# Making the attention gates as one more projection block, turned afterwards, in a two-layer hybrid decoder step on one core

## What is computed

```python
def nsa_project(h, pos, w_in, b_gate, g_q, g_k):
    z = h @ w_in
    q = z[..., :NSA_QD].reshape(B, T, NSA_HEADS, HEAD_DIM)          # 1024 columns
    kv = z[..., NSA_QD:NSA_QD + 6 * NSA_KVD].reshape(...)           # 1536 columns
    gates = jax.nn.sigmoid((z[..., NSA_QD + 6 * NSA_KVD:] + b_gate).astype(jnp.float32))   # 48 columns
    q = partial_rope(rms_norm(q, g_q), pos)
    ...
```

## Times and profile before

| | us |
|---|---|
| median of 3 executions | 2009.44 |
| lowest, highest | 2008.98, 2014.61 |
| the profiled execution | 2014.1 |
| its span, first to last instruction | 2012.3 |
| PE busy in it | 1832.8 (91%) |
| DVE, ACT, POOL busy | 895.4, 677.2, 444.4 |
| mean granted PE clock, of full | 0.929 |

### The profile page before, as it was taken

The page is one execution under the profiler, slowest core; times in us unless marked ns, Lnnn a source line. Parts: engine busy times, 40 slices in busy tenths (PEclk is TensorE's granted clock), DMA queues, the critical chain, the costliest instruction groups (busy, mean ns, idle before and its releaser), DMA issues.

```text
span 2012.3 us, 32814 instructions
## 1 busy us (share of the span) xinstructions
PE 1832.8 (91%) x13711; PEld 1661.6 (83%) x13711; DVE 895.4 (44%) x1345; ACT 677.2 (34%) x1129; POOL 444.4 (22%) x380
## 2 busy tenths in 40 slices
PE   4999997999999997999799999788876999999996
PEld 2989876999999997889678878566653999999996
DVE  6060254744434455546522422777522644444343
ACT  3243333332323233232333321666652331313130
POOL 3344224100000003433222121576812100000000
PEclk8999767999999998999898898799997999999998
DMA  4122122222222221322312110000283122222211
GB/s 158 43 84 84 45 88 88 108 102 85 84 85 84 85 89 45 106 74 95 126 53 84 43 53 1 1 1 9 91 339 149 57 113 103 107 85 85 85 43 43
DMA packets 22255, 166.28 MB, mean 83 GB/s; under 512 B 2112, under 2 KB 9840, under 8 KB 12568
## 3 DMA queue, kind: packets, MB, share of 16 engines
q1 hardware_dynamic: 17896, 122.60, 16.4%
q0 software_dynamic: 4208, 41.45, 5.5%
HBM read 154.00 MB, written 10.04 MB: 82 GB/s over the span
## 4 chain that ended last, share of the span: by engine, by line
PE 79%; DVE 9%; ACT 4%; POOL 3%; issue 2%; DMA 2%; ACTq 0%; DVEq 0%; SPq 0%; PEldq 0%; POOLq 0%
PE slot L2029 51%; PE slot L2253 11%; POOL phase L908 3%; PE slot L2240 2%; PE slot L2001 2%; PE slot L2103 1%; ACT phase L1349 1%; PE slot L2135 1%; DVE normed_x L1460 1%; PE slot L2064 1%; PE slot L2376 1%; DVE phase L1444 1%; PE slot L2436 1%; PE slot L2081 1%; DVE phase L1861 1%
## 5 line engine op out<-in xcount | busy, mean ns | idle before, releaser
L1179 ACT ACTIVATE w_high<-weights 128x1024 fp32r<-128x1024 f32 x128 | 135.3, 1060 | 258.1 <-PE slot L2029 250.0
L2029 PE MATMUL slot<-h_high,w_high 128*128 128x260 f32 x1024 | 209.6, 286 | 6.6 <-issue 6.6
L2029 PE MATMUL slot<-h_high,w_rest 128*128 128x260 f32 x1024 | 209.3, 286 | 5.6 <-issue 5.6
L2029 PE MATMUL slot<-h_rest,w_high 128*128 128x260 f32 x1024 | 208.4, 285 | 0.0
L2029 PE MATMUL slot<-u_high,w_high 128*128 128x260 f32 x1024 | 206.3, 283 | 0.0
L2029 PE MATMUL slot<-u_rest,w_high 128*128 128x260 f32 x1024 | 206.1, 283 | 0.0
L2029 PE MATMUL slot<-u_high,w_rest 128*128 128x260 f32 x1024 | 206.0, 283 | 0.0
L1640 DVE TENSOR_TENSOR w_rest<-weights,w_high 128x1024 fp32r<-128x1024 f32 x128 | 156.0, 1222 | 31.1 <-ACT w_high L1179 31.1
L2029 PEld LDWEIGHTS slot<-h_high,w_high 128*128 128x128 f32 x1024 | 160.4, 191 | 10.8 <-issue 10.5
L2029 PEld LDWEIGHTS slot<-h_high,w_rest 128*128 128x128 f32 x1024 | 160.2, 191 | 3.1 <-issue 3.1
L2029 PEld LDWEIGHTS slot<-h_rest,w_high 128*128 128x128 f32 x1024 | 160.0, 191 | 0.0
(11 more groups left out here) (354 smaller groups left out, 3780.5 us busy)
## 6 DMA issues: line engine op xcount, KB each, us to landing
weights<-in_wt SPq DMA_DIRECT2D x47, 2048.0 KB, 8.6
weights<-in_state SPq DMA_DIRECT2D x2, 2048.0 KB, 8.7
out<-weights POOLq DMA_DIRECT2D x2, 2048.0 KB, 8.7
weights<-in_w SPq DMA_DIRECT2D x2, 2048.0 KB, 9.0
phase<-in_v_win SPq DMA_DIRECT2D x4, 1024.0 KB, 6.9
out<-phase SPq DMA_DIRECT2D x6, 512.0 KB, 6.5
phase<-in_x_prompt SPq DMA_DIRECT2D x2, 1024.0 KB, 6.3
weights<-in_k_win SPq DMA_DIRECT2D x2, 1024.0 KB, 7.1
```

Source lines behind the costliest of these rows:

```text
L1179: nc.scalar.activation(w_part[k % 4][0][:, :, :], ring[:, s, :, 128 * (k % 4):128 * (k % 4) + 128], ACT.Copy).then_inc(w_high_ready, 1)
L2029: last = mm(ps[0:w.shape[2], a, 0:HT], w[:, k, :], m[:, k, HT * a:HT * a + HT], start=k == 0 and w is high and m is x_high, stop=k == DC - ...
```

## The change

The gates become a 21st block of the projection, 48 outputs wide: ACT and POOL split `wgate` into the two `pw_part[0]` buffers, PE makes "gt" with 48 matmuls of 260 columns from `u_part`, ACT copies the [48, 520] result to `z4`, and PE turns it back with five transposes ("gates") into the form that it had. Both stand after sw(18) and nm(19); "gt" comes before sw(19), "gates" after it. Since `u_part` is now read until gt is through, the first cache rows go where `hT` lay (free once the split tokens are made), the first gather moves up to step 6 of the projection, and the rounded compression weights go to `no` in exchange.

```diff
-        rows16 = [cols("no", 0, 4096), W(0, 4096)]
+        rows16 = [cols("hT", 0, 4096), W(0, 4096)]
-        w1_part = [part("w1_high", at["hT"][0], 16, 256), part("w1_rest", at["ring"][0], 16, 256)]
+        w1_part = [part("w1_high", at["no"][0], 16, 256), part("w1_rest", at["ring"][0], 16, 256)]
...
                 if n < len(chunks):
                     yield "z", n
-                elif n == len(chunks):
-                    yield "gates", 0
                 if 0 <= n - 2 < len(chunks) and is_roped[n - 2]:
                     yield "sw", n - 2
                 if 0 <= n - 1 < len(chunks) and is_roped[n - 1]:
                     yield "nm", n - 1
+                if n >= len(chunks) and n < len(chunks) + 2:
+                    yield ("gt", "gates")[n - len(chunks)], 0
...
# POOL
+                if n == len(chunks):
+                    nc.gpsimd.tensor_tensor(pw_part[0][1][:, :, 0:48], wgate, pw_part[0][0][:, :, 0:48].bitcast(F32),
+                                            ALU.subtract).then_inc(pw_rest_ready, 1)
+                    return
...
-                if what == "z" and n + 2 < len(chunks):
+                if what == "z" and n + 2 <= len(chunks):
                     projection_rest(n + 2)
+                    if n == 6:
+                        pool.wait_ge(mixed_rest_ready[0], DC)
+                        pool.wait_ge(mixed_rest_ready[1], DC)
+                        pool.wait_ge(rows_known, 1)
+                        rows_load(0)
...
-                elif what == "gates":
-                    pool.wait_ge(rows_known, 1)
-                    last_z = where(("z", len(chunks) - 1))
-                    pool.wait_ge(full[last_z[0]], last_z[1] + 1)
-                    rows_load(0)
+                elif what == "gt":
+                    pool.wait_ge(full[where(("gt", 0))[0]], where(("gt", 0))[1] + 1)
...
                     if (r, sp) == (0, 2):
                         pool.wait_ge(roped, turned[len(chunks)])
+                        pool.wait_ge(full[where(("gates", 0))[0]], where(("gates", 0))[1] + 1)
                         rows_load(1)
# ACT
+                if n == len(chunks):
+                    act.wait_ge(nsa_small_in, 32)
+                    nc.scalar.activation(pw_part[0][0][:, :, 0:48], wgate, ACT.Copy).then_inc(pw_high_ready, 1)
+                    return
...
             root_of(len(chunks) - 1, k_roots)
+            ps, fr = await_product(act, ("gt", 0))
+            act.wait_ge(roped, turned[len(chunks) - 3])
+            nc.scalar.activation(halves(z4[0:48, 0, :]), tok(ps)[0:48, :, :], ACT.Copy).then_inc(z_ready, 1)
+            act.wait_ge(z_ready, len(chunks) + 1)
+            act.sem_inc(fr, 1)
# PE
+                elif what == "gt":
+                    pe.wait_ge(pw_rest_ready, len(chunks) + 1)
+                    ps, fu = claim(pe, ("gt", 0))
+                    split_products(ps, [w[:, :, 0:48] for w in pw_part[0]], u_part).then_inc(fu, 1)
                 elif what == "gates":
-                    pe.wait_ge(nsa_small_in, 32)
+                    pe.wait_ge(z_ready, len(chunks) + 1)
                     ps, fu = claim(pe, ("gates", 0))
                     for t in range(5):
                         rows = 128 if t < TT else NS
-                        for k in range(DC):
-                            last = mm(ps[0:rows, 0, 48 * t:48 * t + 48], hT[:, k, 128 * t:128 * t + rows], wgate[:, k, :],
-                                      start=k == 0, stop=k == DC - 1)
+                        last = nc.tensor.transpose(ps[0:rows, 0, 48 * t:48 * t + 48], z4[0:48, 0, 128 * t:128 * t + rows],
+                                                   ident[0:48, 0:48])
                     last.then_inc(fu, 1)
```

More of the change, by code:

```diff
@@ L510, in trunk @@
         for what, n in steps():
-            product((what, n), {"z": n % 2, "nm": 2, "sw": 3, "tok": 3, "gates": 0}[what])
+            product((what, n), {"z": n % 2, "nm": 2, "sw": 3, "tok": 3, "gt": 0, "gates": 1}[what])
         def compression_steps():
@@ L1254, in _ @@
                 act.sem_inc(fr, 1)
-                if n + 2 < len(chunks):
+                if n + 2 <= len(chunks):
                     projection_high(n + 2)
@@ L1272, in _ @@
                             if kv == 0:
-                                act.wait_ge(full[0], where(("gates", 0))[1] + 1)
+                                act.wait_ge(full[0], where(("gt", 0))[1] + 1)
                         if kv:
```

## The result

The changed kernel took 1994.88 us (median of 9 executions, 1991.22 to 2002.50), the kernel before 2009.44 (9 executions beside it, 2001.38 to 2017.80): ratio 0.9939, 95% interval 0.9918 to 0.9959. Four later groups of runs gave the kernel before 2010.46, 2009.18, 2010.89 and 2008.41 us, and the changed kernel once more 1994.68, ratio 0.9925 (0.9903 to 0.9946).

The account below looks back on a forecast made before the run. It took PE's row of work, four fifths of the span, as the bound; 7.9 us gained at full clock less 2.05 for half rate gave 5.85, so 2003.6 us from 2009.44, range 2000 to 2009.5.

Parts of the forecast that it names:

- Removed, added, laid open: End of projection: 11.35 us of gates removed, 5.76 added, 5.0 idle before sw(18); gain 7.9 at full clock.
- What the clock takes back: After the wait before sw(18), PE runs at half rate for 4.1 us of dense work, losing 2.05 us.
- The first compression products: Start of compression: 5.3 us at half rate as before, costing 2.65 us, left unchanged in the sum.
- the second rival: Clock better, 0.22: idle wait does not lower it (2001.5), or it stays up into the compression (1999 to 2001).
- the 13 transposes: Before compression: five gate and eight cache-row transposes; whether they raise the clock, worth up to 2.65 us, was left a rival.
- Hidden work: During projection: ACT's rounding 0.4 to 0.5 us, POOL's subtraction some 0.9 and gather about 1.2 delay nobody.
- The sum: Whole program: 7.9 less 2.05 gives 5.85 us gained, so 2003.6 us.
- the rivals: Beside the forecast (0.50): better clock 0.22, late recovery 0.18, change not doing what it says 0.03, slower 0.07.
- 80 PE entries: End of projection: the old gates' entries on PE, counted as 11.35 us removed from the path.

Follow-up runs that it names:

- a_again: The changed kernel itself measured once more, nothing altered, in a later group of runs; 1994.68 us, ratio 0.9925 to the kernel before.
- a_gt_early: The changed kernel with the new gt block one place earlier, between nm(18) and sw(18); 1997.37 us, ratio 0.9935 to the kernel before.
- a_slot224: The changed kernel with the head of PE's second MLP loop at slot 224; 2001.51 us, ratio 0.9961 to the kernel before.
- b_place: The kernel before with only the place of the gates changed, the old 40 matmuls behind nm(19); 2009.87 us, ratio 1.0008.

## Why the prediction was wrong

**Removed, added, laid open: right.** PE waits 5.02 us ahead of sw(18) (5.0 predicted), gt takes 5.79 (5.76), no wait over 1 us stands before sw(19), and the last sum comes 16.97 us behind nm(18) (17.3 by the sum).

**What the clock takes back: right.** Half rate from the end of the wait, over after 3.8 us of dense work (4.1 taken). `a_again` shows the scatter of this term: gt took 6.44 us there.

**The first compression products: the term was left at its value before.** I took 5.46 us again. They took 4.33, and 4.69 in `a_again`: 0.8 to 1.1 us of the 2.65 of the second rival. In `a_gt_early` they took 5.46 again, and 4.80 and 5.46 in the two kernels with the split block, which don't differ there. So part of this is scatter; what decides it was not isolated, and the question of the 13 transposes stays open.

**Hidden work: right.** ACT's rounding took 0.52 (0.4 to 0.5), POOL's rest 1.03 (0.9), the gather 1.05 (1.2), and none of it shows in PE's row of work.

**The sum: the step that failed.** It said that what starts earlier "moves all that follows", so that the local gain is the gain of the program. It lacks a term, and none of the rivals holds it either. The removed "80 PE entries" were counted as time alone; they are also places in PE's program. The second MLP's loop moved by some 54 of them, and two stops of 5.0 and 6.0 us vanished. In runs this term is 7.4 us, as much as the whole local part (7.8 by runs, 5.85 predicted).

**Where it could have been read.** The page shares out 2% of the chain to "issue", the same before and after, so this row would not have told it. Two other rows of the same page do (count, busy us and mean ns, then the idle time before and what ended it):

```profile
L2029 PE MATMUL slot<-h_high,w_high 128*128 128x260 f32 x1024 | 209.6, 286 | 6.6 <-issue 6.6
L2029 PE MATMUL slot<-h_high,w_rest 128*128 128x260 f32 x1024 | 209.3, 286 | 5.6 <-issue 5.6
```

These 12.2 us of PE standing still in the MLPs' products, waiting for nothing that the profile shows, were there to be asked about. The lists of waits say where: PE waits four times by issue in each MLP, two gaps at every back edge, and behind three of the four edges the clock falls to 0.50. The sign was not to be had from these rows, for none of them gives the slot of the head. Moving a head can bring a stop as well as remove one, as `a_slot224` shows; this belonged into the range on both sides, some 8 us each way.

## What to carry to other kernels

Look for waits by "issue" at the back edges of long unrolled loops before costing any edit: an edit that adds or removes instructions ahead of such a loop can switch them on or off, hundreds of microseconds from the edit. To measure what an edit itself does, fix the loop's place (or hint its closing branch) in both kernels; here that alone gave 5 to 9 us per loop, as much as a careful rearrangement did. A block with 48 outputs costs PE as much as one with 128 (5.79 us against 5.76), and was still cheaper than the same product with the 48 columns moving, which took 11.35 us before and 8.91 in `b_place`. Much of that difference is the clock. The window of the kernel before in which the old gates ran at the full clock, in the columns of the earlier trace rows:

```profile
943.00:946.70 3.70, 3.70 (x36) 3.70 (x35) 2.96 (x1) 0.69 (x1) 1.52 (x2) 1.00 0.43 84
```

That is 0.103 us for an entry, so my estimate for all 80 at the full clock is 8.2 us: some 2.4 of the 5.6 us between the old gates and the new block come from the form itself, the rest from work at the lower clock.

## What the runs showed of the hardware that was not expected

A PE loop of some 1,578 entries closes in 0.21 to 0.24 us with its head at slot 32 or 208 of a block of 256, and takes 3.8 to 4.4 us with it at slot 220 or 224. Each loop that stops brings 18 packets of 16.4 KB more, nine in each of its two further passes and spread over them: its whole body is fetched again.

A pass without a stop takes 92.3 us in every trace. With a stop it takes 3.0 to 6.0 us more, over the 24 stops of these traces. PE's idle time is 2.5 to 3.5 us of it, in two gaps of 0.5 to 2.5. To it comes what the clock does: behind 12 of the stops it stayed full (3.0 to 3.9 us lost), and behind the other 12 PE ran 3.4 or 6.8 us at the lower level of 1.2 GHz (4.5 to 6.0 lost).

A hint for the branch removes stop and packets, where the loader placed the heads and with both at slot 224; with it a body that touches eight blocks is kept whole.
